# Spacing GpSimd's look-ups of weight rows over more units, and adding prior gates two columns at a time, in a PEER expert stage

## The reference, cut to what matters

```python
def _peer(hn, w_query, sub_keys, expert_u, expert_v):      # 1024 tokens, D = 1024
    q = (hn @ w_query).reshape(B, S, PEER_HEADS, 2, PEER_HALF)          # 8 heads
    s = einsum('bshpd,hpkd->bshpk', q, sub_keys)
    ...                                  # top 16 of each half, then the top 16 of their sums
    expert = e1 * N_KEYS + e2            # 8 heads * 16 experts for each token
    gate = jax.nn.softmax(cv, axis=-1)
    ...
        u = expert_u[it]
        pre = einsum('tkd,td->tk', u, xt)
        act = gelu(pre, approximate=False) * gt
        return einsum('tk,tkd->td', act, expert_v[it])
```

## Time and profile before

| | us |
|---|---|
| median of 3 runs | 3867.58 |
| the profiled execution's own time | 3880.33 |
| its span, from first to last instruction | 3878.8 |
| TensorE busy in the span | 3628.0 (94%) |
| VectorE busy | 2680.8 (69%) |
| GpSimd busy | 1850.6 (48%) |
| ScalarE busy | 1248.0 (32%) |

### The profile page before, as it was taken

The page is one execution under the profiler, slowest core; times in us unless marked ns, Lnnn a source line. Parts: engine busy times, 40 slices in busy tenths (PEclk is TensorE's granted clock), DMA queues, the critical chain, the costliest instruction groups (busy, mean ns, idle before and its releaser), DMA issues.

```text
span 3878.8 us, 55417 instructions
## 1 busy us (share of the span) xinstructions
PE 3628.0 (94%) x19324; PEld 3137.7 (81%) x19324; DVE 2680.8 (69%) x5241; ACT 1248.0 (32%) x1831; POOL 1850.6 (48%) x1496
## 2 busy tenths in 40 slices
PE   8989799998998899999999999999999995799999
PEld 6854488887876678899999999999777884578887
DVE  5443377775222348658888999997997662589897
ACT  3013343442111221233333333333334331333333
POOL 1024122231100106868888888678888888212220
PEclk9989899999999999999999999999999997899999
DMA  3249500001220133469899899885889995899997
GB/s 117 97 164 398 211 20 19 9 19 69 77 73 11 38 113 92 83 201 282 284 286 281 279 282 283 274 283 175 275 267 278 295 284 100 301 372 400 382 391 267
DMA packets 349345, 788.63 MB, mean 203 GB/s; under 512 B 110112, under 2 KB 218656, under 8 KB 315296
## 3 DMA queue, kind: packets, MB, share of 16 engines
q1 hardware_dynamic: 210208, 451.28, 34.7%
q0 software_dynamic: 139008, 336.01, 27.6%
HBM read 643.09 MB, written 144.05 MB: 203 GB/s over the span
## 4 chain that ended last, share of the span: by engine, by line
PE 27%; POOL 16%; DVE 7%; DMA 5%; issue 5%; DVEq 1%; ACT 1%; SPq 0%; POOLq 0%; ACTq 0%
PE peer_ps L2128 17%; POOL gates_d L2107 13%; PE peer_ps L2219 5%; PE peer_ps L2142 4%; DMA peer_hid<-gates_d 4%; DMA peer_gat<-gates_d 2%; POOL peer_gates L2102 2%; DVE peer_acc L2541 1%; POOL late_rows L2087 1%; DVEq L2435 1%; PE peer_ps L2165 1%; DVE peer_ul L2422 1%; ACT peer_uh L2315 0%; DVE peer_rows L2526 0%; DVE peer_al L2560 0%
## 5 line engine op out<-in xcount | busy, mean ns | idle before, releaser
L2107 POOL DMA_INDIRECT gates_d<-peer_gates,peer_idx x768 | 1201.2, 1564 | 339.3 <-issue 184.8
L2128 PE MATMUL peer_ps<-high,peer_uh 128*128 128x384 f32 x2048 | 522.0, 335 | 10.8 <-DVE peer_ul L2422 5.0
L2128 PE MATMUL peer_ps<-low,peer_uh 128*128 128x384 f32 x2048 | 520.7, 335 | 0.0
L2128 PE MATMUL peer_ps<-high,peer_ul 128*128 128x384 f32 x2048 | 520.4, 334 | 0.0
L2128 PEld LDWEIGHTS peer_ps<-high,peer_uh 128*128 128x128 f32 x2048 | 369.4, 188 | 14.9 <-issue 7.9
L2128 PEld LDWEIGHTS peer_ps<-high,peer_ul 128*128 128x128 f32 x2048 | 370.6, 188 | 0.0
L2128 PEld LDWEIGHTS peer_ps<-low,peer_uh 128*128 128x128 f32 x2048 | 370.6, 188 | 0.0
L2219 PE MATMUL peer_ps<-peer_vh,peer_ah 128*128 128x512 f32 x1026 | 321.5, 395 | 22.5 <-DVE peer_al L2560 22.4
L2087 POOL DMA_INDIRECT late_rows<-in_expert_uv,peer_idx x108 | 142.1, 1316 | 402.3 <-DVE peer_acc L2541 349.8
L2219 PE MATMUL peer_ps<-peer_vh,peer_al 128*128 128x512 f32 x1026 | 318.3, 391 | 0.0
L2219 PE MATMUL peer_ps<-peer_vl,peer_ah 128*128 128x512 f32 x1026 | 318.2, 391 | 0.0
(11 more groups left out here) (473 smaller groups left out, 7680.8 us busy)
## 6 DMA issues: line engine op xcount, KB each, us to landing
peer_raw<-in_expert_uv SPq DMA_DIRECT2D x170, 512.0 KB
gates_d<-mla_zeros POOLq DMA_DIRECT2D x128, 512.0 KB
hidden_d<-peer_hid SPq DMA_DIRECT2D x128, 384.0 KB, 3.7
peer_raw<-in_expert_u SPq DMA_DIRECT2D x86, 512.0 KB, 5.4
first_raw<-in_expert_uv SPq DMA_DIRECT2D x86, 512.0 KB, 5.1
peer_act_in<-hidden_d SPq DMA_DIRECT2D x171, 192.0 KB, 5.2
peer_gat<-gates_d SPq DMA_DIRECT2D x171, 192.0 KB, 6.0
first_raw<-in_expert_u SPq DMA_DIRECT2D x42, 512.0 KB
```

Of the source, the lines that this page charges most:

```text
L2107: pool.indirect_dma_start(gates_flat, bass.IndirectOffsetOnAxis(ap=idx[:, n, k:k + 1], axis=0), gates[:, n, k:k + 1], None, compute_op=ALU ...
L2128: last = nc.tensor.matmul(ps[i][:, a, 0:HD], w[:, cols], x[:, kc, a * HD:(a + 1) * HD], start=(kc == 0 and w is uh[i % 2] and x is high), ...
```

## The change

Two edits. The look-ups' plan becomes a table of points between which it is interpolated: 119 look-ups are out at the end of unit 23, 148 at the end of unit 29 (before: at the end of unit 27), and the plan from unit 31 on is as before. And the addition ahead of a scatter is made for columns k and k + 1 together, ahead of even columns alone, so that a summed unit has 8 additions instead of 16. The scatters, the look-ups and VectorE's slots stay as they are.

```diff
 SUMMED = 4
+COLUMNS = 2
+ROWS_BY = ((7, 0), (24, 119), (30, EARLY_SLOTS), (31, EARLY_SLOTS), (45, EARLY_SLOTS + PASS_SLOTS))
 FIRST_UNIT = 3
...
         def rows_by(i, k):
 
-            if i < 7:
-                return 0
-            if i < 31:
-                return min(EARLY_SLOTS, EARLY_SLOTS * ((i - 7) * TOPK + k + 1) // (21 * TOPK))
-            return EARLY_SLOTS + (min(PASS_SLOTS, PASS_SLOTS * ((i - 31) * TOPK + k + 1) // (14 * TOPK)))
+            done = i + (k + 1) / TOPK
+            return int(np.interp(done, [x for x, _ in ROWS_BY], [y for _, y in ROWS_BY]))
...
-                    if summed(n):
-                        nc.gpsimd.tensor_tensor(gates[:, n, k:k + 1], gates[:, n, k:k + 1],
-                                                earlier_sum[:, tile - PASSES[1][0], head - 1, k:k + 1], ALU.add
+                    if summed(n) and k % COLUMNS == 0:
+                        nc.gpsimd.tensor_tensor(gates[:, n, k:k + COLUMNS], gates[:, n, k:k + COLUMNS],
+                                                earlier_sum[:, tile - PASSES[1][0], head - 1, k:k + COLUMNS], ALU.add
                                                 ).then_inc(sum_made, 1)
                         sums_made += 1
                         pool.wait_ge(sum_made, sums_made)
```

## The result

The changed kernel takes 3851.19 us (median of six runs, 3845.34 to 3862.08) against 3868.09 us for the kernel before, measured beside it (3866.78 to 3882.13). The ratio of the runs is 0.9944, 95% interval 0.9925 to 0.9963; the two medians alone give 0.9956. Forecast were 3847.5 us, 0.9948 of the median shown. A second session gave 0.9938 (0.9919 to 0.9958).

The account below looks back on a forecast made before the run. GpSimd's list of scatters was taken to set the second pass' start; of about 33 us saved, 13 are given back at look-up 148, leaving 6.4 + 13.7 = 20.1 us off the 3867.58 median: 3847.5 us, range 3832 to 3864.

Parts of the forecast that it names:

- Part 1: GpSimd's additions, 144 become 72: each one removed saves 0.38 us, 27.4 us in total, bounds 14.4 and 28.7.
- Rival 2: Shared port's wait moves to GpSimd's next instruction: only 0.20 us saved per addition, gain 9.3 us, 3858.3 us; chance 0.17.
- Part 2: Units 24 to 26: 14 look-ups instead of 21 shorten head 0's waits for landed scatters by 6 us, bounds 0 and 15.2.
- Part 3: Last blocks in: look-up 147's row lands late, VectorE's low part follows late, and TensorE is held up 19.1 us.
- d: TensorE's hold-up in the last blocks in, waiting for the low part of weights: 19.1 us, bounds 9.4 and 29.4.
- The fall of the clock: TensorE's clock falling for one block behind a stall: up to 8.3 us more, all of it off the gain.
- Part 4: Look-up 148: GpSimd stands still 13 us until TensorE ends its blocks in, and leaves 6.4 us earlier than before.
- Part 5: From look-up 148 to the last scatter: another 13.7 us of sums saved, no wait for used buffers.
- the room at used buffers: Look-up 162, the closest to waiting for a used buffer: 47.8 us of room before, 9 left after the change.
- Sum: Total gain: 6.4 us at look-up 148 plus 13.7 us behind it, 20.1 us, giving 3847.5 us.
- Rival 3: Slower: look-up 148 waits longer than all sums behind it save, from d = 39 us; d = 50 gives 3878.6; chance 0.08.
- Rival 1: Early rows not late enough: d under 6 us, look-up 148 finds TensorE done, whole 33.4 us gained, 3834 us; chance 0.15.

Follow-up runs that it names:

- Old pace: Changed kernel, but with the old interleaving of look-ups up to unit 23 and the new plan from unit 24 on; 0.9921 of the kernel before.
- Late start: Changed kernel with the first late look-up one unit later (plan point 31 becomes 32); 0.9912 of the kernel before.
- later slots: Changed kernel with VectorE's slots for the last early rows one and two later; 0.9914 of the kernel before.
- spread one: Changed kernel with one 16-column sum for a unit, late look-ups in units 32 to 45, VectorE's last early-row slots one and two later; 0.9871 of the kernel before.
- sums whole: Changed kernel with one 16-column sum for a unit, 9 sums instead of 72; 0.9917 of the kernel before.

## Why the prediction was right, point by point

- **What bounds the kernel.** Right. The second pass started 9.5 us behind the last scatter (9.6 before), and 9.4 to 9.8 in all variants, and the end followed.
- **Part 1, sums.** Taken: 27.4 us in all, 0.38 each. The sums alone gave 27.8. Rival 2, the port's wait moving on, is refuted by the scatters' unchanged length. The rule it was drawn from, the exclusive lock of VectorE and GpSimd in the Trainium skill ("SBUF — State Buffer", section on the two separate sides), is not itself contradicted, only the inference that the lock's wait would move on to the next instruction.
- **Part 2, head 0's waits.** Undersized: 6 us taken, 13.2 measured (29.6 to 16.4), near the bound of 15.2. GpSimd's waits in units 24 to 26, kernel after (compare):

```profile
POOL gates_d L2106 <- DMA gates_d<-peer_gates,peer_idx: 16.4, 6, 4.6
```

- **Not seen: the plan also moved the look-ups of units 7 to 23.** The prediction said that 119 were out at the end of unit 23 either way and priced this at nothing. But the old plan put them at drifting columns, the new at fixed ones, and unit 23 then ends 9.6 us later (2444.5 against 2439.0 us in the trace, and 4.1 for the earlier first scatter). The undersized waits of part 2 give back 7.2 of it, and other pauses in units 24 to 26 fell from 6.4 us, 4.4 of them two waits for used buffers, to 1.8. So GpSimd's arrival at look-up 148 came out near, 22.5 us earlier against 19.7, partly by luck: one term put at nothing and others set too low nearly cancel. Old pace shows besides that the terms are tied: without the 9.6 us, units 25 and 26 take them back.
- **Part 3, late rows.** Right in its mechanism, the last row decides, and sized too high: d was 19.1, measured 13.4. Look-up 147 came 42.4 us later than before instead of 47.4, and its product could start 6.9 us behind it instead of 7.7; these two are the difference. The fall of the clock, named as a risk that would come off the gain, did come, but ahead of the last wait, and so it added nothing to d.
- **Part 4, the wait at look-up 148.** Right: 11.45 us against 13. It left 11.4 us earlier than before instead of 6.4, because TensorE was ready earlier. (The prediction calls what stands behind it "7 units' scatters and more"; it is half of unit 31 and 16 units.) Late start and later slots each removed the wait. Late start got more than its worth back, later slots 6 to 7 us.
- **Part 5.** 13.7 taken, 12.6 measured, as a sum of two. Up to unit 44 GpSimd gained 18.5 us, 16.2 of them in sums, which took 440 ns each there before; then 5.9 were given back in units 45 to 47. Scatters of those units, kernel before, then after:

```profile
L2107 POOL DMA_INDIRECT gates_d<-peer_gates,peer_idx x48 | 79.5, 1655 | 14.6 <-issue 14.6
```
```profile
L2106 POOL DMA_INDIRECT gates_d<-peer_gates,peer_idx x48 | 85.4, 1778 | 14.6 <-issue 14.6
```

Before, more than half of these ran while TensorE and VectorE stood idle for the gates (1.55 us each, as the scatter in the earlier trace rows). Coming earlier, more of them run beside VectorE's work. In the other versions their mean is 1745 to 1801 ns, and 1861 in the spread one. That is a tax on the gains here.

- **Part 5, the room at used buffers.** "No wait" was right, but the room was not 9 us. VectorE frees row 156's buffer at the end of the first of two additions, at 2933.5, and GpSimd issues look-up 162 at 2935.5, kernel after (compare):

```profile
2932.20 2.69 DVE L2540 SCALAR_TENSOR_TENSOR peer_acc<-late_rows,peer_pre,peer_acc 128x1024 f32<-128x1024 f32 x2
...
2935.49 1.87 POOL L2086 DMA_INDIRECT late_rows<-in_expert_uv,peer_idx  x1 [0.30 <-issue]
```

That is 2.0 us (3.1 in the changed kernel's second trace): GpSimd came 28.9 us earlier there, not 20, and VectorE 16.9 later. The changed kernel stands at the edge of the next limit, which sums whole then met.

- **Sum.** 20.1 forecast, 24.1 measured in the traces, 17 to 24 by the medians and ratios. The main terms are right, and the luck lies in those that make up GpSimd's arrival at look-up 148. (Rival 3's case of d = 50 adds up to 3878.4, not 3878.6.) Rival 1 (rows not late) and rival 3 (slower) did not occur. The plan alone is a loss: the gain is the sums'.

What stays open is why fixed columns lengthen units 9 to 23. The lengthening repeats within 0.4 us in the seven traces that share this part of the plan, and old pace takes it away, so it is no noise. That it is an alignment with VectorE's order of work is not shown; no run measured which of VectorE's instructions stand beside which scatters.

## What to carry to other kernels

When an engine's list is thinned, look for the next instruction on it that waits for another engine: half of what is saved ahead of it may only lengthen that wait (here 11 of 22 us), and moving one such instruction a little down the list can get it back. Then work out the room at the wait behind it: the changed kernel had 2 us left at its buffers, and the next saving of 14 us behind look-up 148 was mostly lost there. A spreading of prefetches has a price on the consumer's side, so move the consumer's slots with it. And measure combined edits one at a time: here one was worth 26 us and the other cost 4 to 9, and the pair hid it.

## What the runs showed of the hardware

- TensorE's clock fell to its lower level for some microseconds behind waits of 2.1 and 4.9 us in the blocks in (granted clock 0.78 from 2611.4 to 2624 us). The length of a wait alone does not decide it: in the changed kernel's second trace a wait of 2.4 us was followed by the lower clock and later ones of 2.0, 2.1 and 2.4 us were not (granted clock 1.00 from 2635 to 2645 us, behind the one of 2.1). In the kernel before, waits of up to 1.7 us there left the granted clock at 1.00.
- A GpSimd addition of 16 columns takes hardly more than one of a single column: the shortest take 0.23 and 0.19 us. The means are 0.35, 0.41, 0.52 and 0.46 us in the four versions with nine such additions, and 0.40 with 144 of one column (kernel before). So at this size it is in the main a price for the instruction.
- An indirect DMA's time on GpSimd goes with what VectorE does. Of the accumulating scatters of units 36 to 47 in the kernel before, the 41 with no VectorE instruction beside them took 1.55 to 1.58 us; the 65 with VectorE busy beside them for over nine tenths of their time took 1.93 us on average, and up to 2.62.
